# A four-layer diffusion step on one Trainium2 core: where VectorE scales a finished attention output unit in the MLA layers

## The chip, the cores and the metric

The kernel runs on one core of a Trainium2 chip. The metric is the device time of one execution in microseconds (us), the median of several runs. The engines are named as in the profile: PE is TensorE (its matmuls), PEld its weight loads, DVE is VectorE, ACT is ScalarE, POOL is GpSimd, SP is the engine that issues most DMAs. Each engine works through its own queue in order and meets the others through semaphores.

## The reference, cut to what matters

Four layers run one after another on 256 context tokens and 1024 latent tokens, with token mixer `i % 3` in layer i: multi-head latent attention (MLA) in layers 0 and 3, grouped-query attention in layer 1, windowed attention in layer 2. The change touches only the attention of the MLA layers:

```python
def mla_attend(q_nope, q_rope, k_nope, k_rope, v):
    scale = (MLA_NOPE + MLA_ROPE) ** -0.5
    def attend(qn, qr):
        s = (jnp.einsum('bqhd,bkhd->bhqk', qn, k_nope, preferred_element_type=F32)
             + jnp.einsum('bqhr,bkr->bhqk', qr, k_rope, preferred_element_type=F32)) * scale
        p = jax.nn.softmax(s, axis=-1)
        return jnp.einsum('bhqk,bkhd->bqhd', p.astype(v.dtype), v)
    return sweep_queries(attend, (q_nope, q_rope))
...
def finish(o, gate, w_out):
    B, T = o.shape[:2]
    return (o.reshape(B, T, BRANCH) * jax.nn.silu(gate)) @ w_out
```

There are 16 heads. Latent queries read 512 cached, 1024 latent keys; context queries read the 256 context keys.

## The kernel before

`attention` runs one layer's 16 heads in pairs: `pairs_of_heads` writes out the first and the last pair and loops over the six between. In a pair, b is 0 for the first head and 1 for the second. A head has three units of queries: unit 0 and unit 1 are 512 latent queries each, unit 2 is the 256 context queries. The keys are taken in steps of 1024 columns: steps 0 to 5 belong to unit 0, steps 6 to 11 to unit 1, step 12 to unit 2. So a head has NS = 13 steps, a pair P2 = 26.

In step p each engine does, in this order:

- PE: the six score matmuls of step p (L1653), one matmul of the next head's maxima (an "entry", L1461 in `emit_entry`), the six P·V matmuls of step p-2 (L1624 to L1628), and the step's other entries.
- ACT: exp of the scores to `p_f` in float32 (L1711) and again to `p_hi` in float16 (L1715). When a unit's last P·V is done, Ln and Exp make `recip_den`, the reciprocal of the softmax denominators (L1731, L1733), two steps after the unit's last step.
- DVE: the maximum of the step's first entry (L1506 in `take_entry`), then `p_lo` = `p_f` - `p_hi` of step p-1 (L1783), then the maxima of the other entries, and in three of the 13 steps `normed`: `o_f` = the unit's P·V sum times `recip_den` (L1763). In steps 5, 7 and 10 POOL makes `p_lo` in DVE's place (L1856).
- POOL: for each finished unit the gate product (L1838), its float16 part (L1842) and the rest (L1844).

The entries prepare the next head: 26 row maxima of 512 or 256 score columns, three "turns" in which a unit's negated maxima are transposed into the next head's query rows (L1488, copied by ACT at L1538), and, in layer 0 alone, one entry for the next layer's adaLN weights (L1478 or L1426). They are spread over steps 2 to 12 and write two half banks in turn, so an entry's matmul waits until DVE has taken the entry two places earlier. I call the entry with number k "entry k": in layer 0 step 8 holds entries 18, 19, 20, step 9 holds 21, 22 and the turn 23, and step 10 begins with entry 24. In both MLA layers step 2 holds entries 0, 1, 2, and step 3 begins with 3. Entries 0 and 1 are the 256-column maxima of the context queries; entry 1 closes their group, so two small instructions follow it (L1510, L1517).

`normed(i, p)` scales unit 0 in step 8, unit 1 in step 1 of the next head and unit 2 in step 2 of the next head. It waits for `recip_den` and, through `s_og`, for POOL to be done with the `o_f` buffer of two units before. For the second head of a pair it writes partitions 64 to 127 (`rows = slice(HD * b, HD * b + HD)`), for the first head partitions 0 to 63. Its result releases POOL's L1838 and, through `s_o`, the P·V bank and the `recip_den` buffer for the unit after next.

In the MLA layers the order of DVE in a step before was:

```python
take_entry(first) ; p_lo(p - 1) ; take_entry(others) ; normed(i, p)
```

Of the kernel before, what the change touches and what calls it, by code (L numbers as in the profile page):

```python
# [64 lines left out]
def above_zero(value):  # L65

    return not isinstance(value, int) or value > 0
# [19 lines left out]
class Program:  # L87
# [1135 lines left out]
    def attention(self, kind, Q, K, ada_layer, nxt):  # L1223
# [6 lines left out]
        mla, swa = kind == 0, kind == 2  # L1230
# [158 lines left out]
        def pairs_of_heads(eng, body):  # L1389

            if mla:
                peeled(eng, NB, body)
            else:
                for i in range(NB):
                    body(i, i == 0, i == NB - 1)
# [33 lines left out]
        def take_ada(dve, mb, group):  # L1429

            out = A[:, at(group * 3, 3), :]
            dve.tensor_tensor(out, mb[:, 0:6].rearrange("p (r c) -> p r c", r=3),
                              ada_bias[:, at(group * 3, 3)].unsqueeze(2).to_broadcast([P, 3, 2]), ALU.add
                              ).then_inc(s_at.h, 1)
# [56 lines left out]
        def take_entry(dve, hd, b, k):  # L1491
            e = entries[k]
            if e[0] == "ada" and b == 0 and above_zero(hd):
                dve.wait_ge(s_me.h, s_me.base + hd * NE + k + 1)
                take_ada(dve, MB[(b * NE + k) % 2], hd // 2 - 1)
            if e[0] == "ada" and b == 1:
                if above_zero(hd - 1):
                    dve.wait_ge(s_at.h, s_at.base + hd // 2)
                dve.wait_ge(s_me.h, s_me.base + hd * NE + k + 1)
                dve.tensor_copy(rows, MB[(b * NE + k) % 2][:, 0:3 * P]).then_inc(s_ar.h, 1)  # L1500
            if e[0] != "max":
                return
            _, u, t, c, k0, n, masks = e
            par = (3 * b + turn_order[u]) % 2
            dve.wait_ge(s_me.h, s_me.base + hd * NE + k + 1)
            dve.tensor_reduce(mx[:, par, t, c:c + 1], MB[(b * NE + k) % 2][:, 0:n], AX.X, ALU.max).then_inc(s_red.h, 1)  # L1506
            nt = units[u][1] // P
            if t == nt - 1 and c == parts[u] - 1:
                dve.wait_ge(s_red.h, s_red.base + hd * NM + nmax[k + 1])
                dve.tensor_reduce(m4[:, par, 0:nt], mx[:, par, 0:nt, 0:parts[u]], AX.X, ALU.max).then_inc(s_m4.h, 1)  # L1510
                o = turn_order[u]
                dve.wait_ge(s_m4.h, s_m4.base + hd * 3 + o + 1)
                if swa:
                    dve.tensor_scalar(negm[:, par, 0:nt], m4[:, par, 0:nt], sink_raw[:, at(hd)], -1.0 / MAX_UNIT,
                                      ALU.max, ALU.mult).then_inc(s_neg.h, 1)
                else:
                    dve.tensor_scalar(negm[:, par, 0:nt], m4[:, par, 0:nt], -1.0 / MAX_UNIT, None, ALU.mult  # L1517
                                      ).then_inc(s_neg.h, 1)

        def sink_lo(dve, hd, b, o):  # L1520

            q0, nq = units[next(u for u in range(3) if turn_order[u] == o)]
            dve.wait_ge(s_eh.h, s_eh.base + hd * 3 + o + 1)
            dve.tensor_tensor(erow[32:33, b, q0:q0 + nq], es_row[o], erow[0:1, b, q0:q0 + nq], ALU.subtract
                              ).then_inc(s_el.h, 1)
# [19 lines left out]
        with nc.Block() as block:  # L1545
# [192 lines left out]
            @block.vector  # L1738
            def _(dve):
                if swa:  # L1740
                    dve.tensor_scalar(sink_raw[:], sink, 1.0 / scale, None, ALU.mult).then_inc(s_raw.h, 1)
                    dve.wait_ge(s_raw.h, s_raw.base + 1)
                for k in range(NE):
                    take_entry(dve, 0, 0, k)

                def normed(i, p):

                    e = p - 3
                    if e < 0 and i_first[0]:
                        return  # L1750
                    q = e % P2
                    u = steps[q % NS][0]
                    if q % NS != last_of[u]:
                        return
                    un = 3 * (q // NS) + u if e >= 0 else 3 * (q // NS) + u - 6
                    b = q // NS
                    nq = units[u][1]
                    dve.wait_ge(s_rd.h, s_rd.base + i * 6 + un + 1)

                    if above_zero(i * 6 + un - 1):  # L1760
                        dve.wait_ge(s_og.h, s_og.base + i * 6 + un - 1)
                    rows = slice(HD * b, HD * b + HD)
                    dve.tensor_tensor(o32[rows, un % 2, 0:nq], OB[un % 2][0:HD, 0:nq], rden[rows, un % 2, 0:nq],  # L1763
                                      ALU.mult).then_inc(s_o.h, 1)
                i_first = [True]

                def body(i, first, last):
                    i_first[0] = first
                    for p in range(P2 + (3 if last else 0)):
                        b = p // NS  # L1770
                        found = at_step[p % NS] if p < P2 and not (last and p >= NS) else []
                        for k in found[:early]:
                            take_entry(dve, i * 2 + b + 1, 1 - b, k)
                        if p <= P2 and not (first and p == 0) and (p - 1) % P2 % NS not in pooled:

                            q = (p - 1) % P2
                            cols = steps[q % NS][2]
                            g = i * P2 + p - 1
                            dve.wait_ge(s_ph.h, s_ph.base + g + 1)

                            if above_zero(g - back[q] + 1):
                                dve.wait_ge(s_av.h, s_av.base + g - back[q] + 1)
                            dve.tensor_tensor(pl[:, slot[q], 0:cols], p32[:, q % 2, 0:cols], ph[:, slot[q], 0:cols],  # L1783
                                              ALU.subtract).then_inc(s_pl.h, 1)
                        if not mla:
                            normed(i, p)
                        for k in found[early:]:
                            take_entry(dve, i * 2 + b + 1, 1 - b, k)
                        if swa and p < P2:
                            for o in ((0, 1), (2,))[p % NS] if p % NS < 2 else ():  # L1790
                                sink_lo(dve, i * 2 + b, b, o)
                        if mla:
                            normed(i, p)
                    if first:
                        self.next_lo(dve, nx)
                pairs_of_heads(dve, body)
                if ada:
                    dve.wait_ge(s_me.h, s_me.base + HEADS * NE + 1)
                    take_ada(dve, MB[0], KD - 1)
                    dve.wait_ge(s_at.h, s_at.base + KD)  # L1800

                    dve.scalar_tensor_tensor(A[:, KD:2 * KD, :], A[:, KD:2 * KD, :], 1.0,
                                             self.norm_g(ada_layer).unsqueeze(2).to_broadcast([P, KD, 2]),
                                             ALU.add, ALU.mult).then_inc(s_fin.h, 1)
# [321 lines left out]
```

## Time and profile before

| what | value |
| --- | --- |
| runs | 4359.85, 4364.03, 4364.70 us; median 4364.03 us |
| the profiled execution | 4366.46 us, its span 4364.7 us, granted clock 0.959 over the whole span |
| PE busy | 3982.1 us, 91% of the span |
| DVE busy | 2740.2 us, 63% |
| ACT busy | 2399.3 us, 55% |
| POOL busy | 1259.2 us, 29% |
| L1506, maxima on DVE | 1536 instructions, 967.5 us |
| L1783, `p_lo` on DVE | 624 instructions, 757.3 us |
| L1763, `o_f` on DVE | 192 instructions in four layers, 48 in each |

A row of the timeline reads: start, duration, engine, source line, operation, tile written and tile read, shape, count, and in brackets how long the engine sat idle before and what ended that. A pipelined matmul is shown as lasting 0.38 us although the next starts 0.215 us after it, so short pauses of PE do not show as idle time; they are read from the distance between the starts. Layer 0's attention fills about 550 to 1150 us of the span, layer 3's about 3620 to 4240 us.

### The profile page before, as it was taken

Reading aid. Unit: us, or ns where it says so; the run is one execution under the profiler, and the core shown is the slowest. Engines: PE = TensorE matmul, PEld = TensorE weight load, DVE = VectorE, ACT = ScalarE, POOL = GpSimd, SP = SyncE. Lnnn points to the kernel's source line nnn. Section 1 sums busy time; section 2 is a strip of 40 time slices with the busy share of each in tenths; the row PEclk is TensorE's granted clock in tenths of the full one; section 3 lists DMA queues with packets and bytes.
Section 4 is the critical chain, followed back from the end, with each engine's and each line's share of the span. In section 5 each row is a group of like instructions: output and inputs, shape, how many; then the busy total and the mean of one; then the engine's idle time right before and its main releaser. Section 6 shows DMA issues by size and latency. Waiting matters only on the chain. (4 is left out here: it accounts for less than half of the span.)

```text
span 4364.7 us, 58626 instructions
## 1 busy us (share of the span) xinstructions
PE 3982.1 (91%) x20892; PEld 1947.8 (45%) x20892; DVE 2740.2 (63%) x3651; ACT 2399.3 (55%) x3166; POOL 1259.2 (29%) x875
## 2 busy tenths in 40 slices
PE   5997799999999989999999988888999779999998
PEld 1453244444445544444445544444455324444444
DVE  4315477777555738888845528888542447777754
ACT  3325377777634328777833217778332437777761
POOL 1001034434321204444422103333210103444442
PEclk8998799999999989999999989999999879999999
DMA  4124522322202332222111432332111361221211
GB/s 195 49 79 132 161 62 65 76 62 65 73 14 65 116 101 56 62 65 57 45 61 51 123 107 64 83 82 54 57 43 64 110 188 37 55 48 42 54 34 62
DMA packets 375904, 329.39 MB, mean 75 GB/s; under 512 B 247584, under 2 KB 295264, under 8 KB 374544
## 3 DMA queue, kind: packets, MB, share of 16 engines
q1 hardware_dynamic: 375696, 326.60, 26.8%
q8 instruction: 133, 2.18, 0.2%
q14 instruction: 75, 0.61, 0.0%
HBM read 235.30 MB, written 91.23 MB: 75 GB/s over the span
## 5 line engine op out<-in xcount | busy, mean ns | idle before, releaser
L1506 DVE TENSOR_REDUCE max_parts<-bank 128x1 f32<-128x512 f32 (+2 forms) x1536 | 967.5, 656 | 278.7 <-PE bank L1461 254.6
L726 PE MATMUL bank<-H_hilo,w_hilo 128*128 128x512 f16 (+1 forms) x5832 | 1065.7, 346 | 12.4 <-DVE w_hilo L968 8.1
L1711 ACT ACTIVATE p_f<-bank 128x1024 f32<-128x1024 f32 (+2 forms) x768 | 741.3, 965 | 534.0 <-PE bank L1653 487.4
L1653 PE MATMUL bank<-q_slots,k_slots 96*128 96x512 f16 (+7 forms) x3968 | 937.6, 365 | 0.7 <-ACT p_hi L1715 0.6
L1783 DVE TENSOR_TENSOR p_lo<-p_f,p_hi 128x1024 f16<-128x1024 f32 (+2 forms) x624 | 757.3, 1216 | 162.0 <-ACT p_hi L1715 159.0
L726 PEld LDWEIGHTS bank<-H_hilo,w_hilo 128*128 128x128 f16 x5832 | 572.7, 98 | 504.1 <-issue 16.2
L1715 ACT ACTIVATE p_hi<-bank 128x1024 f16<-128x1024 f32 (+2 forms) x768 | 738.3, 961 | 0.0
L1461 PE MATMUL bank<-k_slots,q_slots 96*128 96x512 f16 (+4 forms) x1536 | 542.0, 382 | 111.4 <-DVE max_parts L1506 62.7
L1624 PE MATMUL bank<-p_hi,v_hi_ones 128*128 128x512 f16 (+2 forms) x1568 | 565.3, 362 | 31.1 <-DVE p_lo L1783 18.6
L1626 PE MATMUL bank<-p_hi,v_lo_zeros 128*128 128x512 f16 (+2 forms) x1568 | 565.6, 361 | 0.0
L1628 PE MATMUL bank<-p_lo,v_hi_ones 128*128 128x512 f16 (+2 forms) x1568 | 564.3, 361 | 0.0
L1653 PEld LDWEIGHTS bank<-q_slots,k_slots 96*128 96x128 f16 (+2 forms) x3968 | 375.4, 98 | 397.6 <-issue 24.9
L1838 POOL TENSOR_TENSOR o_gated<-o_f,gate_rows 64x512 f32<-64x512 f32 (+1 forms) x192 | 236.3, 1231 | 846.3 <-DVE o_f L1763 640.2
L1856 POOL TENSOR_TENSOR p_lo<-p_f,p_hi 128x1024 f16<-128x1024 f32 x144 | 316.3, 2197 | 533.6 <-ACT p_hi L1715 510.2
L931 ACT ACTIVATE z_ring<-bank 128x512 f32<-128x512 f32 x328 | 148.7, 531 | 510.3 <-PE bank L726 496.9
L968 DVE SCALAR_TENSOR_TENSOR w_hilo<-w_f,w_hilo 128x1024 f16<-128x1024 f32 (+2 forms) x93 | 114.0, 1227 | 339.0 <-ACT w_hilo L894 337.9
L1461 PEld LDWEIGHTS bank<-k_slots,q_slots 96*128 96x128 f16 (+1 forms) x1536 | 150.4, 98 | 368.4 <-DVE max_parts L1506 168.3
L1049 POOL TENSOR_TENSOR var_rstd<-z_ring,sin 128x1280 f32<-128x1280 f32 x14 | 47.5, 3393 | 662.9 <-ACT z_ring L931 515.0
L1844 POOL TENSOR_TENSOR H_hilo<-o_gated,H_hilo 64x512 f16<-64x512 f32 (+3 forms) x192 | 231.6, 1206 | 23.6 <-POOL H_hilo L1842 13.9
L1624 PEld LDWEIGHTS bank<-p_hi,v_hi_ones 128*128 128x128 f16 x1568 | 152.4, 97 | 191.4 <-DVE p_lo L1783 46.1
L1628 PEld LDWEIGHTS bank<-p_lo,v_hi_ones 128*128 128x128 f16 x1568 | 152.5, 97 | 159.4 <-issue 1.1
L1626 PEld LDWEIGHTS bank<-p_hi,v_lo_zeros 128*128 128x128 f16 x1568 | 153.1, 98 | 141.1 <-issue 0.8
(173 smaller groups left out, 3620.2 us busy)
## 6 DMA issues: line engine op xcount, KB each, us to landing
ada_w<-in_w_ada SPq DMA_DIRECT2D x48, 768.0 KB, 5.7
gate<-z_ring SPq DMA_DIRECT2D x32, 640.0 KB, 2.9
gate_rows<-gate SPq DMA_DIRECT2D x64, 320.0 KB, 4.0
q_slots<-q_mla SPq DMA_DIRECT2D x64, 240.0 KB, 3.2
k_mla<-hilo_out SPq DMA_DIRECT2D x64, 224.0 KB
k_slots<-k_mla SPq DMA_DIRECT2D x64, 224.0 KB, 4.3
v_hi_ones<-v_scratch SPq DMA_DIRECT2D x64, 224.0 KB, 2.9
v_lo_zeros<-v_scratch SPq DMA_DIRECT2D x64, 224.0 KB, 3.5
```

The lines of the kernel that those rows point to most:

```text
L726: ins = pe.matmul(dst, lhs(a, k), rhs(b, k), start=(k == 0 and n == 0), stop=(k == nk - 1 and n == 2))
L1461: ins = pe.matmul(mb[:, 0:n], Q[0:kk, q_slot(hd, b), 0, q0:q0 + P], K[0:kk, k_slot(hd, b), 0, k0:k0 + n], start=True, stop=True)
L1506: dve.tensor_reduce(mx[:, par, t, c:c + 1], MB[(b * NE + k) % 2][:, 0:n], AX.X, ALU.max).then_inc(s_red.h, 1)
L1624: pe.matmul(d, V[:, b, kt], ph[:, slot[q], sel], start=first and n == 0, stop=False, skip_group_check=True)
L1626: pe.matmul(d, VL[:, b, kt], ph[:, slot[q], sel], start=False, stop=False, skip_group_check=True)
L1628: ins = pe.matmul(d, V[:, b, kt], pl[:, slot[q], sel], start=False, stop=fin, skip_group_check=True)
L1653: ins = pe.matmul(dst, lhs, rhs, start=(m == 0), stop=(m == len(ops) - 1), skip_group_check=swa)
L1711: act.activation(p32[:, p % 2, 0:cols], src, ACT.Exp, scale=scale).then_inc(s_p32.h, 1)
L1715: act.activation(ph[:, slot[p], 0:cols], src, ACT.Exp, scale=scale).then_inc(s_ph.h, 1)
L1783: dve.tensor_tensor(pl[:, slot[q], 0:cols], p32[:, q % 2, 0:cols], ph[:, slot[q], 0:cols], ALU.subtract).then_inc(s_pl.h, 1)
L1838: pool.tensor_tensor(og[rows, 0:nq], o32[rows, s, 0:nq], G[rows, q0:q0 + nq], ALU.mult).then_inc(s_og.h, 1)
L1856: pool.tensor_tensor(pl[:, slot[p], 0:cols], p32[:, p % 2, 0:cols], ph[:, slot[p], 0:cols], ALU.subtract).then_inc(s_pp.h, 1)
```

## The change

In `body` of the DVE program, `normed(i, p)` in the MLA layers moves from behind the step's other maxima to the place ahead of them. The other two layers have that order already.

```diff
@@ -1782,15 +1782,12 @@
                             dve.tensor_tensor(pl[:, slot[q], 0:cols], p32[:, q % 2, 0:cols], ph[:, slot[q], 0:cols],
                                               ALU.subtract).then_inc(s_pl.h, 1)
-                        if not mla:
-                            normed(i, p)
+                        normed(i, p)
                         for k in found[early:]:
                             take_entry(dve, i * 2 + b + 1, 1 - b, k)
                         if swa and p < P2:
                             for o in ((0, 1), (2,))[p % NS] if p % NS < 2 else ():
                                 sink_lo(dve, i * 2 + b, b, o)
-                        if mla:
-                            normed(i, p)
```

On DVE, in step 8 of a head (between the `p_lo` of step 6 and that of step 8; the row of five maxima is entries 16 to 20, the single one entry 21):

```order
 L1783 TENSOR_TENSOR p_lo<-p_f_6,p_hi 128x1024 [waits s_pv,s_p_hi]
-L1506 TENSOR_REDUCE max_parts<-bank 128x1 [waits s_max_entry] x5
+L1506 TENSOR_REDUCE max_parts<-bank 128x1 [waits s_max_entry] x3
 L1763 TENSOR_TENSOR o_f_6<-bank,recip_den 64x512 [waits s_rden]
-L1506 TENSOR_REDUCE max_parts<-bank 128x1 [waits s_max_entry]
+L1506 TENSOR_REDUCE max_parts<-bank 128x1 [waits s_max_entry] x3
 L1783 TENSOR_TENSOR p_lo<-p_f_6,p_hi 128x1024 [waits s_pv,s_p_hi]
```

`o_f` of unit 0 now stands behind entry 18 and ahead of entries 19 and 20, which are followed at once by entry 21 and the `p_lo` of step 8.

On DVE, in step 2 of the next head (from the `p_lo` of step 1 to that of step 2; the maxima are entries 1, 2 and 3):

```order
 L1783 TENSOR_TENSOR p_lo<-p_f_6,p_hi 128x1024 [waits s_pv,s_p_hi]
-L1506 TENSOR_REDUCE max_parts<-bank 128x1 [waits s_max_entry]
-L1510 TENSOR_REDUCE max_rows<-max_parts 128x2 [waits s_max_part]
-L1517 TENSOR_SCALAR neg_max<-max_rows 128x2 [waits s_max_row]
-L1506 TENSOR_REDUCE max_parts<-bank 128x1 [waits s_max_entry]
 L1763 TENSOR_TENSOR o_f_6<-bank,recip_den 64x256 [waits s_o_gated,s_rden]
 L1506 TENSOR_REDUCE max_parts<-bank 128x1 [waits s_max_entry]
+L1510 TENSOR_REDUCE max_rows<-max_parts 128x2 [waits s_max_part]
+L1517 TENSOR_SCALAR neg_max<-max_rows 128x2 [waits s_max_row]
+L1506 TENSOR_REDUCE max_parts<-bank 128x1 [waits s_max_entry] x2
```

`o_f` of unit 2 now comes straight behind `p_lo`, ahead of entry 1 with its two small instructions and ahead of entry 2. Unit 1's `o_f` (step 1, in which there are no entries) keeps its place, and so does every instruction of PE, ACT, POOL and SP.

## Rows read from the trace of the kernel before

**Rows 1.** Busy time by engine, one stretch of layer 0: PE, PEld, DVE, ACT, POOL, clock, DMA.

```profile
655.00:764.00 109.00, 108.54 (x536) 48.54 (x534) 85.46 (x128) 78.46 (x95) 46.22 (x34) 1.00 0.28 65
```

**Rows 2.** The line L1763 in layer 0: who waited for it, us and times.

```profile
who waited for it (us, times):
  POOL o_gated L1838: 169.6, 30
```

**Rows 3.** Timeline of PE, layer 0, second head of a pair: steps 8 to 10.

```profile
675.87 0.38 PE L1461 MATMUL bank<-k_slots,q_slots 96*128 96x512 f16 x1
...
677.82 1.46 PE L1653 MATMUL bank<-q_slots,k_slots 96*128 96x512 f16 x6
679.12 0.38 PE L1461 MATMUL bank<-k_slots,q_slots 96*128 96x512 f16 x1
...
681.26 1.48 PE L1653 MATMUL bank<-q_slots,k_slots 96*128 96x512 f16 x6
682.89 0.39 PE L1461 MATMUL bank<-k_slots,q_slots 96*128 96x512 f16 x1 [0.15 <-DVE max_parts L1506]
```

**Rows 4.** Timeline of DVE, the same place.

```profile
676.29 0.69 DVE L1506 TENSOR_REDUCE max_parts<-bank 128x1 f32<-128x512 f32 x1 [0.23 <-PE bank L1461]
677.80 1.29 DVE L1506 TENSOR_REDUCE max_parts<-bank 128x1 f32<-128x512 f32 x2 [0.82 <-PE bank L1461]
679.12 0.68 DVE L1763 TENSOR_TENSOR o_f<-bank,recip_den 64x512 f32<-64x512 f32 x1
679.84 0.69 DVE L1506 TENSOR_REDUCE max_parts<-bank 128x1 f32<-128x512 f32 x1
680.56 1.67 DVE L1783 TENSOR_TENSOR p_lo<-p_f,p_hi 128x1024 f16<-128x1024 f32 x1
682.15 0.68 DVE L1506 TENSOR_REDUCE max_parts<-bank 128x1 f32<-128x512 f32 x1
```

**Rows 5.** Timeline of POOL, the same place.

```profile
679.88 1.26 POOL L1838 TENSOR_TENSOR o_gated<-o_f,gate_rows 64x512 f32<-64x512 f32 x1 [2.76 <-DVE o_f L1763]
681.31 1.39 POOL L1842 CAST H_hilo<-o_gated 64x512 f32 x1 [0.17 <-POOL o_gated L1838]
```

**Rows 6.** Timeline of ACT, the same place: the reciprocal that `o_f` waits for.

```profile
675.48 0.63 ACT L1733 ACTIVATE recip_den<-recip_den 64x512 f32<-64x512 f32 x1
```

**Rows 7.** Timeline of PE, layer 0, next head (first of its pair): step 10.

```profile
721.67 1.48 PE L1653 MATMUL bank<-q_slots,k_slots 96*128 96x512 f16 x6
723.17 0.39 PE L1461 MATMUL bank<-k_slots,q_slots 96*128 96x512 f16 x1
```

**Rows 8.** Timeline of PE, layer 0, step 10 of the second and the fifteenth head.

```profile
599.65 0.38 PE L1653 MATMUL bank<-q_slots,k_slots 97*128 97x512 f16 x1
...
600.68 0.39 PE L1461 MATMUL bank<-k_slots,q_slots 96*128 96x512 f16 x1 [0.65 <-DVE max_parts L1506]
...
1130.07 1.48 PE L1653 MATMUL bank<-q_slots,k_slots 96*128 96x512 f16 x6
1131.72 0.39 PE L1461 MATMUL bank<-k_slots,q_slots 96*128 96x512 f16 x1 [0.18 <-DVE max_parts L1506]
```

**Rows 9.** Timeline, layer 3, steps 1 to 4, as unit 2 of a second head is scaled.

```profile
3768.15 1.23 DVE L1783 TENSOR_TENSOR p_lo<-p_f,p_hi 128x1024 f16<-128x1024 f32 x1 [0.29 <-ACT p_hi L1715]
...
3768.46 0.41 ACT L1733 ACTIVATE recip_den<-recip_den 64x256 f32<-64x256 f32 x1
...
3769.30 0.41 DVE L1506 TENSOR_REDUCE max_parts<-bank 128x1 f32<-128x256 f32 x1
...
3770.16 0.38 PE L1461 MATMUL bank<-k_slots,q_slots 96*128 96x512 f16 x1
...
3770.75 0.42 DVE L1763 TENSOR_TENSOR o_f<-bank,recip_den 64x256 f32<-64x256 f32 x1
...
3771.33 0.72 POOL L1838 TENSOR_TENSOR o_gated<-o_f,gate_rows 64x256 f32<-64x256 f32 x1
...
3771.93 1.22 DVE L1783 TENSOR_TENSOR p_lo<-p_f,p_hi 128x1024 f16<-128x1024 f32 x1
...
3773.81 0.39 PE L1461 MATMUL bank<-k_slots,q_slots 96*128 96x512 f16 x1 [0.17 <-DVE max_parts L1506]
```

## The prediction, made before the changed kernel was run

> **What bounds the kernel now.** I read the busy time by stretch first. In MLA's attention PE is busy 108.5 of 109 us at full granted clock, DVE 85.5, ACT 78.5, POOL 46.2 [rows 1]. So PE sets the time, and the change, which touches DVE alone, can be worth only what PE loses by waiting for DVE. Second, I ask who waits for the moved instruction: in layer 0 only POOL, 30 times, 169.6 us [rows 2], and POOL has that time to spare; PE is not in the list. An earlier `o_f` is therefore worth nothing by itself. What can count is what stands behind it on DVE. PE's pauses are shorter than the 0.16 us by which a shown matmul overlaps the next, so I took the distance from a step's first score matmul to its first entry. Undisturbed it is 679.12 - 677.82 = 1.30 us (six matmuls of 0.217 us) [rows 3]. In layer 0's step 10 it is 682.89 - 681.26 = 1.63, a pause of 0.33 that ended when DVE had taken entry 22 (682.15 + 0.68 = 682.83) [rows 3, 4]. With the head in the other half of the pair it is 723.17 - 721.67 = 1.50, a pause of 0.20 [rows 7].
>
> **Why entry 22 is late.** `o_f` begins at 679.12 and entry 21, whose matmul began at 679.12 as well, is taken only at 679.84. An entry is otherwise taken 676.29 - 675.87 = 0.42 after its matmul starts, so DVE could have had it at 679.54: 0.30 us lost behind `o_f` [rows 3, 4]. Then `p_lo` of step 8 takes 1.67 instead of the 1.23 of a free one [rows 4, 9], because POOL's L1838, released by `o_f`, runs from 679.88 to 681.14 [rows 5]: 681.14 + 1.23 = 682.37 against the end that is shown, 682.23. DVE is held until about 0.14 before the POOL instruction's end and then needs its 1.23.
>
> **Step 8 after the change, layer 0.** Entry 18 is taken by 676.29 + 0.69 = 676.98 [rows 4]. `recip_den` was ready at 675.48 + 0.63 = 676.11 [rows 6], so `o_f` does not wait: 677.01 to 677.69. DVE was idle for 0.82 us there until entry 19 came at 677.80 [rows 4]; the 0.68 of `o_f` fit, with 0.11 to spare. Entries 19 and 20 keep their times, to 679.09. Entry 21: 679.54 to 680.22. POOL starts 2.1 us earlier: L1838 at about 677.77 to 679.03, the cast L1842 (1.39, after 0.17) at 679.20 to 680.59 [rows 5]. `p_lo` of step 8 then starts at 680.14, in the cast's tail. The trace has no `p_lo` that starts under a cast, so two bounds: free, it ends at 681.37; held as under L1838, at 680.59 - 0.14 + 1.23 = 681.68. I take the second, the nearest row being L1838's. Entry 22 is taken by 682.28 at the latest, and PE would need it at 681.26 + 1.30 = 682.56. The pause goes altogether, with over 0.2 us in hand, also in the case of 0.20, where by the same steps entry 22 is done at about 722.6 and PE asks at 722.97.
>
> On this pairwise blocking the Trainium skill ("SBUF — State Buffer", "Who interferes with whom") says that a VectorE instruction with two SBUF inputs and a GpSimd instruction that reads SBUF exclude each other for a whole instruction, whoever starts first. The trace agrees for L1838 with the 1.67 [rows 4, 5]; by that page the cast blocks too, and the sum is the same by it, since both bounds close the pause.
>
> There are 15 such places in layer 0 (the last head prepares no successor). One is larger, 600.68 - 599.65 - 0.22 = 0.81, the last is 1131.72 - 1130.07 - 1.30 = 0.35 [rows 8]; six read about 0.32 as in [rows 3] and seven 0.20 or a little over, as in [rows 7]. Sum: 0.81 + 0.35 + 6 x 0.32 + 7 x 0.21 = 4.5 us. Downstream, scores, exponentials and maxima of steps 10 to 12 all start from PE, so they move forward with it and I expect nothing of it to be given back.
>
> **Step 8 in layer 3.** Without the adaLN entry the numbering is shifted: the turn is entry 21, and step 10's first entry waits for a turn that ACT copies, not for a maximum behind `p_lo`. I found no pause of PE at that entry in any of the 15 places. Gain 0.
>
> **Step 2, both layers.** Here the move delays something. The `p_lo` before it ends at 3768.15 + 1.23 = 3769.38, `recip_den` is ready at 3768.87, and `o_f` (0.42) goes ahead of entry 1 [rows 9]. For a second head, `o_f` starts 0.03 us after the instruction before it has ended and so does the one behind it (679.09 to 679.12, 679.80 to 679.84 [rows 4]), while `p_lo` to entry 1 overlap by 0.08 [rows 9]. So entry 1 is done at 3769.38 + 0.03 + 0.42 + 0.03 + 0.41 = 3770.27 instead of 3769.71; with 0.06 us for the signal (682.83 to 682.89 [rows 3, 4]) PE starts entry 3 at 3770.33 instead of 3770.16: 0.17 us late. It costs little, because in these heads PE stops again a step later, at entry 6, until DVE has taken entry 4 (3773.81 [rows 9]), and that moment is DVE's own: DVE has the same work between the `p_lo` of step 1 and that of step 2 in either order, so that `p_lo` starts at 3771.93 or up to 0.13 earlier, and POOL's L1838 (3771.33 to 3772.05; it starts 0.16 after `o_f` ended instead of the 0.08 of [rows 4, 5], so it waited for POOL's own work and does not move) holds it to 3772.05 - 0.14 + 1.23 = 3773.14, where it ends now (3773.15). In first heads, without the 0.03s and with the overlap kept, entry 1 comes 0.42 - 0.08 = 0.34 later, less than the slack of 3770.16 - 3769.71 - 0.06 = 0.39: nothing. Bounds: 0, and 0.17 x 14 = 2.4 us if the later stop does not swallow it. I take 0.
>
> On the 0.03 us: the Trainium skill ("VectorE: DVE Perf Modes", "Two Vector instructions with no wait between them") has a Vector instruction held until all earlier ones have finished when its output starts in another quadrant of partitions than the last. That is the second head's `o_f`, and the trace agrees with the 0.03 against the overlap of 0.08 [rows 4, 9]. By a rule without it the delay of entry 3 would be about 0.02, and the sum above would not change.
>
> **Sum.** The profiled execution took 4366.5 us; 4366.5 - 4.5 = 4362.0. It lies 2.4 above the median of the runs shown, so for the median 4364.0 - 4.5 = 4359.5 us.
>
> **Rivals.**
> 1. Hidden anyway, no gain. The pause at entry 24 goes but PE meets another within the head, or the `p_lo` of step 8 is held longer than the cast. For it: a pause that is gone brings PE sooner to whatever DVE finishes last next. Against it: what DVE does next (entries 24 and on) starts from PE's own matmuls, which move forward too. Price 0 to +2.4 (the step 2 bound): 4364 to 4366.5.
> 2. Slower: POOL takes the port twice. If, after the cast, POOL's L1844 gets in ahead of the waiting `p_lo` (680.14), and lasts like L1838 (1.26), `p_lo` ends at about 680.59 + 0.17 + 1.26 - 0.14 + 1.23 = 683.1, entry 22 is taken at 683.7, and PE waits 1.2 instead of 0.33: +0.87 x 15 = 13 us in layer 0; I count none in layer 3, where no entry waits behind it. 4364 + 13 = 4377. It decides the matter once `p_lo` ends later than 681.9. Against it: in [rows 4, 5] the `p_lo` that waited under L1838 ran before the cast got its turn, in spite of POOL's pause of only 0.17 between the two.
> 3. Faster: step 2 also improves. If the `p_lo` of step 2, up to 0.13 earlier, gets ahead of POOL's L1838, the stops at entry 6 go too: about 0.33 at each of 15 places in the two layers, 4.9 us. 4359.5 - 4.9 = 4354.6. Against it: `p_lo` would have to start 0.3 earlier.
> That the change does not do what it says can be excluded: the order of DVE's instructions shows it, and only there.
>
> **How the numbers follow.** Chances: forecast 0.66 (4359.5), rival 1 0.22 (4364 to 4366.5), rival 2 0.05 (4377), rival 3 0.07 (4354.6). What a measurement of this kernel can tell from no change is about 0.2%, 8.7 us, hence faster is below 4355.3 and slower above 4372.7. My forecast is a gain of half that size, so "same" is the likely outcome: 0.90; faster 0.05, most of rival 3; slower 0.05, rival 2. Range: from rival 3's 4354.5 to rival 1's upper end, 4367, leaving out rival 2.
>
> **What would show it.** Right: in layer 0's step 10 the distance from the first score matmul to entry 24 falls from 1.63 and 1.50 to 1.30; `o_f` of unit 0 starts right behind entry 18; L1838 starts 2.1 us earlier relative to step 8; the `p_lo` of step 8 lasts 1.23 to 1.6. Entry 3 stands 0.1 to 0.2 later in second heads, and entry 6 where it was. Wrong: a new stop of PE at entry 3 that is not made good by entry 6; a `p_lo` of over 2 us in step 8; or a span of layer 0's attention that is not shorter by 4 to 5 us.

## The result and the profile after

The changed kernel takes 4375.56 us (median of 8 runs, 4370.27 to 4379.46) against 4363.7 us for the kernel before, measured beside it (8 runs, 4359.52 to 4371.18): ratio 1.0026, 95% interval 1.0015 to 1.0037. It is slower by 11.9 us. I had forecast 4359.5, a gain of 4.5 us, with 0.05 on slower.

All of it lies in the attention of the two MLA layers. The line of PE's score matmuls gives the length of each: first and last start of L1653, in the kernel before (layer 0, layer 3) and then in the changed one.

```profile
L1653 PE MATMUL bank<-q_slots,k_slots x1248: 269/379/634, 525.8 to 1171.5; 96*128 96x512 f16 x111, 97*128 97x512 f16 x54, 96*128 96x256 f16 x9, 97*128 97x256 f16 x5
L1653 PE MATMUL bank<-q_slots,k_slots x1248: 270/379/634, 3600.0 to 4234.2; 96*128 96x512 f16 x111, 97*128 97x512 f16 x54, 96*128 96x256 f16 x9, 97*128 97x256 f16 x5
```

```profile
L1653 PE MATMUL bank<-q_slots,k_slots x1248: 269/379/634, 525.1 to 1175.6; 96*128 96x512 f16 x111, 97*128 97x512 f16 x54, 96*128 96x256 f16 x9, 97*128 97x256 f16 x5
L1653 PE MATMUL bank<-q_slots,k_slots x1248: 270/379/634, 3602.6 to 4243.4; 96*128 96x512 f16 x111, 97*128 97x512 f16 x54, 96*128 96x256 f16 x9, 97*128 97x256 f16 x5
```

645.7 + 634.2 = 1279.9 us became 650.5 + 640.8 = 1291.3 us: 11.4 us longer. I use this sum below as "the two stretches". The whole kernel's time differs by several microseconds from run to run, and the stretches leave out what lies outside the attention. But no kernel was profiled twice, and the first head of layer 3 alone takes 40.07 us in one trace and 41.20 in another (the kernel before and e2), so I read nothing into a difference of under 2 us; where less is at stake I go by distances inside the heads.

Now the place that answers to [rows 9], step 2 of layer 3 behind a second head, in the changed kernel: DVE, then POOL, then PE.

```profile
3771.41 1.23 DVE L1783 TENSOR_TENSOR p_lo<-p_f,p_hi 128x1024 f16<-128x1024 f32 x1 [0.29 <-ACT p_hi L1715]
3772.67 0.42 DVE L1763 TENSOR_TENSOR o_f<-bank,recip_den 64x256 f32<-64x256 f32 x1
3773.12 0.42 DVE L1506 TENSOR_REDUCE max_parts<-bank 128x1 f32<-128x256 f32 x1
3773.58 0.15 DVE L1510 TENSOR_REDUCE max_rows<-max_parts 128x2 f32<-128x2 f32 x1
3773.77 0.71 DVE L1517 TENSOR_SCALAR neg_max<-max_rows 128x2 f16<-128x2 f32 x1
3774.39 1.27 DVE L1506 TENSOR_REDUCE max_parts<-bank 128x1 f32<-128x512 f32 x2
3775.58 1.37 DVE L1783 TENSOR_TENSOR p_lo<-p_f,p_hi 128x1024 f16<-128x1024 f32 x1
```

```profile
3773.29 1.15 POOL L1841 TENSOR_TENSOR H_hilo<-o_gated,H_hilo 64x512 f32 x1 [0.18 <-POOL H_hilo L1839]
```

```profile
3772.12 1.46 PE L1653 MATMUL bank<-q_slots,k_slots 96*128 96x512 f16 x6
3773.60 0.39 PE L1461 MATMUL bank<-k_slots,q_slots 96*128 96x512 f16 x1
...
3775.12 0.39 PE L1461 MATMUL bank<-k_slots,q_slots 96*128 96x512 f16 x1
3775.72 0.39 PE L1461 MATMUL bank<-k_slots,q_slots 96*128 96x512 f16 x1 [0.21 <-DVE max_parts L1506]
3775.94 1.46 PE L1653 MATMUL bank<-q_slots,k_slots 96*128 96x512 f16 x6
3777.61 0.39 PE L1461 MATMUL bank<-k_slots,q_slots 96*128 96x512 f16 x1 [0.20 <-DVE max_parts L1506]
```

The row to see is L1517, the negation of two numbers per partition: 0.71 us. It starts at 3773.77, 0.48 us after POOL's third instruction on unit 1 (L1841, L1844 of the kernel before) started, and it ends at 3774.48, 0.04 after POOL's 3774.44. In the kernel before it stood 0.58 us earlier in the step, 0.10 ahead of POOL's, and took 0.17. DVE, then POOL, in the kernel before:

```profile
3769.93 0.17 DVE L1517 TENSOR_SCALAR neg_max<-max_rows 128x2 f16<-128x2 f32 x1
```

```profile
3770.03 1.15 POOL L1844 TENSOR_TENSOR H_hilo<-o_gated,H_hilo 64x512 f32 x1 [0.18 <-POOL H_hilo L1842]
```

Behind a first head the shift is 0.32 us and the negation takes 0.95. After the change DVE is half a microsecond behind: entry 5's matmul comes 3775.72 - 3775.12 - 0.22 = 0.38 late and entry 6's 0.37 (1.67 from the first score matmul instead of 1.30). The stop of entry 6 was there before, 0.33 behind second heads and none behind most first ones; now it is 0.36 behind nearly every head, and layer 3's heads are longer by just what the negation lost: 40.25 us became 40.79 where it takes 0.71 instead of 0.17, and 39.89 became 40.68 where it takes 0.95 (from first score matmul to first score matmul). The group of these negations, 128x2, before and then after (count, busy us, mean ns):

```profile
L1517 DVE TENSOR_SCALAR neg_max<-max_rows 128x2 f16<-128x2 f32 x48 | 16.2, 338 | 1.7
```

```profile
L1517 DVE TENSOR_SCALAR neg_max<-max_rows 128x2 f16<-128x2 f32 x48 | 29.4, 612 | 1.7
```

13.2 us more for 48 instructions, of which 31 lie in the MLA layers. There 23 take 0.54 to 0.78 us longer, and four that had been held for 1.17 us before take 0.33 to 0.58 less. The net is about the size of the loss.

The other place, steps 8 to 10 of a second head of layer 0 (answering to [rows 3 to 5]): DVE, POOL, PE.

```profile
758.06 0.69 DVE L1506 TENSOR_REDUCE max_parts<-bank 128x1 f32<-128x512 f32 x1 [0.23 <-PE bank L1461]
758.78 0.68 DVE L1763 TENSOR_TENSOR o_f<-bank,recip_den 64x512 f32<-64x512 f32 x1
759.57 1.29 DVE L1506 TENSOR_REDUCE max_parts<-bank 128x1 f32<-128x512 f32 x2
761.31 0.69 DVE L1506 TENSOR_REDUCE max_parts<-bank 128x1 f32<-128x512 f32 x1 [0.45 <-PE bank L1461]
762.03 1.97 DVE L1783 TENSOR_TENSOR p_lo<-p_f,p_hi 128x1024 f16<-128x1024 f32 x1
```

```profile
759.54 1.26 POOL L1835 TENSOR_TENSOR o_gated<-o_f,gate_rows 64x512 f32<-64x512 f32 x1 [0.65 <-DVE o_f L1763]
760.97 0.61 POOL L1839 CAST H_hilo<-o_gated 64x512 f32 x1 [0.17 <-POOL o_gated L1835]
761.76 1.16 POOL L1841 TENSOR_TENSOR H_hilo<-o_gated,H_hilo 64x512 f32 x1 [0.18 <-POOL H_hilo L1839]
```

```profile
759.59 1.46 PE L1653 MATMUL bank<-q_slots,k_slots 96*128 96x512 f16 x6
760.89 0.38 PE L1461 MATMUL bank<-k_slots,q_slots 96*128 96x512 f16 x1
...
763.03 1.48 PE L1653 MATMUL bank<-q_slots,k_slots 96*128 96x512 f16 x6
764.65 0.39 PE L1461 MATMUL bank<-k_slots,q_slots 96*128 96x512 f16 x1
```

`o_f` stands where I said, in DVE's idle time behind entry 18, entry 21 is taken 0.42 after its matmul (761.31 after 760.89), and `p_lo` starts 0.30 earlier than before (2.44 after step 9's first score matmul instead of 2.74; I had worked out 0.42). But the cast took 0.61 us, not 1.39. So POOL's third instruction starts at 761.76, ahead of `p_lo`, and holds it: 1.97 us instead of 1.67. Entry 24 comes 1.62 after the first score matmul, as before (1.63). So it is at 12 of the 15 places. At the first two and the last the distance fell, from 1.60, 2.12 and 1.65 to 1.37, 1.31 and 1.43: 1.3 us of the 4.5 that I had forecast.

### The profile page after: what moved, and what is told of

Read it like the earlier page. It is cut to its first block and busy times, and to the rows that moved or that the text cites. A ratio compares the mean times of both kernels' runs of the same rounds, so it can differ in the third digit from the quotient of the medians.

```text
span 4374.2 us, 58626 instructions
## 1 busy us (share of the span) xinstructions
PE 3987.5 (91%) x20892; PEld 1947.8 (45%) x20892; DVE 2752.1 (63%) x3651; ACT 2400.3 (55%) x3166; POOL 1229.2 (28%) x875
## 5 line engine op out<-in xcount | busy, mean ns | idle before, releaser
L1653 PE MATMUL bank<-q_slots,k_slots 96*128 96x512 f16 (+7 forms) x3968 | 938.2, 366 | 0.7 <-ACT p_hi L1715 0.6
L726 PEld LDWEIGHTS bank<-H_hilo,w_hilo 128*128 128x128 f16 x5832 | 571.7, 98 | 501.1 <-issue 10.8
L1653 PEld LDWEIGHTS bank<-q_slots,k_slots 96*128 96x128 f16 (+2 forms) x3968 | 375.7, 98 | 395.1 <-issue 25.0
L1835 POOL TENSOR_TENSOR o_gated<-o_f,gate_rows 64x512 f32<-64x512 f32 (+1 forms) x192 | 225.6, 1175 | 779.8 <-DVE o_f L1763 573.2
L1841 POOL TENSOR_TENSOR H_hilo<-o_gated,H_hilo 64x512 f16<-64x512 f32 (+3 forms) x192 | 256.1, 1334 | 23.6 <-POOL H_hilo L1839 13.9
```

Of the source, the lines that this page charges most:

```text
L726: ins = pe.matmul(dst, lhs(a, k), rhs(b, k), start=(k == 0 and n == 0), stop=(k == nk - 1 and n == 2))
L1653: ins = pe.matmul(dst, lhs, rhs, start=(m == 0), stop=(m == len(ops) - 1), skip_group_check=swa)
L1841: pool.tensor_tensor(H(1), og[rows, 0:nq], H(0), ALU.subtract).then_inc(s_ol.h, 1)
```

## The experiments

The theory from the two traces, A: the loss is the negation L1517, held by POOL's instruction since it starts behind it; unit 0's move gives and costs next to nothing. Rivals: B, the longer hold of step 8's `p_lo` costs the time; C, both parts share it; D, DVE's new order costs by itself (maxima taken later), whatever POOL does. All rows below are medians and ratios to the kernel before measured beside them (a ratio is made from all the runs and need not be that of the two medians); the last column is the two stretches of one profiled execution.

| kernel | us | before, beside it | ratio (95%) | two stretches, us |
| --- | --- | --- | --- | --- |
| before | | | | 1279.9 |
| changed | 4375.56 | 4363.7 | 1.0026 (1.0015 to 1.0037) | 1291.3 |
| e1 unit 2 early | 4380.21 | 4366.5 | 1.0031 (1.0018 to 1.0043) | 1292.7 |
| e2 unit 0 early | 4362.94 | 4366.5 | 0.9993 (0.9984 to 1.0002) | 1279.2 |
| e3 unit 2 in the middle | 4371.54 | 4366.5 | 1.0008 (0.9999 to 1.0017) | 1283.6 |
| e4 both a step later | 4370.64 | 4366.5 | 1.0010 (1.0001 to 1.0019) | 1283.2 |
| e5 changed, unit 1's POOL work cut | 4369.0 | 4366.24 | 1.0002 (0.9992 to 1.0011) | 1280.5 |
| e6 before, the same cut | 4364.35 | 4366.24 | 0.9993 (0.9983 to 1.0002) | 1275.7 |
| e7 unit 0 early, unit 0's POOL work cut | 4361.74 | 4366.24 | 0.9989 (0.9979 to 0.9998) | 1273.9 |
| e8 before, the same cut | 4364.91 | 4366.24 | 0.9998 (0.9988 to 1.0009) | 1279.0 |
| e9 changed, other negation | 4360.85 | 4366.15 | 0.9988 (0.9979 to 0.9997) | 1275.7 |
| e10 before, other negation | 4364.99 | 4366.15 | 0.9997 (0.9989 to 1.0006) | 1276.8 |
| e11 unit 2 a step later | 4361.79 | 4366.15 | 0.9990 (0.9981 to 0.9998) | 1275.8 |
| e12 combined | 4359.61 | 4366.15 | 0.9984 (0.9975 to 0.9993) | 1272.2 |
| e13 before, maximum and negation in one | 4353.29 | 4366.92 | 0.9968 (0.9956 to 0.9980) | 1271.1 |
| e14 combined, and in one | 4347.92 | 4366.92 | 0.9957 (0.9943 to 0.9970) | 1263.1 |

### The two parts apart: e1 and e2

`normed` gets the units it may scale as an argument. In e1 unit 2 alone goes ahead, in e2 unit 0 alone:

```diff
                         if not mla:
                             normed(i, p)
+                        else:
+                            normed(i, p, (2,))      # e2: (0,)
                         for k in found[early:]:
                             take_entry(dve, i * 2 + b + 1, 1 - b, k)
...
                         if mla:
-                            normed(i, p)
+                            normed(i, p, (0, 1))    # e2: (1, 2)
```

> One part of the change alone: in the MLA layers only unit 2's o_f (step 2) goes ahead of the step's other maxima, unit 0's stays behind them. Theory A (the whole loss is in step 2: the 128x2 negation L1517 now starts after POOL's third instruction of unit 1 has started and lasts 0.7 to 0.95 us instead of 0.17): the time of the changed kernel, about 12 us over the kernel before, with L1517 at 0.7 to 0.95 in the trace. Theory B (the loss comes from the longer shadow on the p_lo of step 8, unit 0): no change, 4364. Theory C (both halves share it): 3 to 9 us over.

> The other part alone: only unit 0's o_f (step 8) goes ahead, unit 2's stays behind. Theory A: within 1.5 us of the kernel before; the pauses at entry 24 in layer 0 stay at about 0.31 and 0.19 us because the p_lo of step 8 (1.7 to 2.0 us) is now held by POOL's third instruction instead of its first. Theory B: all of the 12 us. The forecast's own sum would have been -4.5 us.

e1 has the whole loss (1.0031, stretches +12.8 us) and e2 none: stretches -0.7 us, ratio at most 1.0002 by its interval. Its median is 3.6 us under the kernel before, where I had expected 1.5 at most; the interval holds both. B and C fall.

### Between the two: e3

```diff
                         for k in found[early:]:
                             take_entry(dve, i * 2 + b + 1, 1 - b, k)
+                            if mla and k == 1:
+                                normed(i, p, (2,))
```

> Unit 2's o_f goes between the two: behind entry 1 and its two small instructions (L1510, L1517), ahead of entry 2; unit 0's stays behind. Theory A: L1517 keeps its old start, ahead of POOL's third instruction, lasts 0.17 us, and the time is that of the kernel before within 1.5 us. Rival D (any o_f ahead of a maximum in step 2 costs, since entry 2 and with it entry 3 come later): 4 us or more over.

The negation is back at 0.17 us, and most of the loss is gone; but 3.7 us of stretch and 5.0 of the median remain, where theory A had 1.5 at most and rival D 4 or more. The trace of layer 3 behind a first head shows where: DVE, then POOL, then PE.

```profile
3815.15 0.17 DVE L1517 TENSOR_SCALAR neg_max<-max_rows 128x2 f16<-128x2 f32 x1
3815.32 0.42 DVE L1763 TENSOR_TENSOR o_f<-bank,recip_den 64x256 f32<-64x256 f32 x1
3815.66 1.27 DVE L1506 TENSOR_REDUCE max_parts<-bank 128x1 f32<-128x512 f32 x2
3816.86 1.49 DVE L1783 TENSOR_TENSOR p_lo<-p_f,p_hi 128x1024 f16<-128x1024 f32 x1
```

```profile
3816.54 0.73 POOL L1840 TENSOR_TENSOR o_gated<-o_f,gate_rows 64x256 f32<-64x256 f32 x1
```

```profile
3817.43 1.46 PE L1653 MATMUL bank<-q_slots,k_slots 96*128 96x512 f16 x6
3819.01 0.39 PE L1461 MATMUL bank<-k_slots,q_slots 96*128 96x512 f16 x1
```

`p_lo` of step 2 starts 0.32 us after POOL's first instruction on unit 2 (L1838 of the kernel before) and is held, 1.49 us. In the kernel before, at the same place, it started 0.25 after it and it was POOL that waited:

```profile
3811.72 1.21 DVE L1783 TENSOR_TENSOR p_lo<-p_f,p_hi 128x1024 f16<-128x1024 f32 x1
```

```profile
3811.47 2.04 POOL L1838 TENSOR_TENSOR o_gated<-o_f,gate_rows 64x256 f32<-64x256 f32 x1
```

With the other loser of this meeting comes a stop of PE of 3819.01 - 3817.43 - 1.30 = 0.28 us at entry 6, behind the first heads of layer 3, whose lengths grew by 0.30. The start alone does not settle who loses: with 0.25 us between the two starts the kernel before has eight meetings in the MLA layers that `p_lo` won and one that it lost (742.07, 1.55 us), while at 0.28 us and over it lost in every run. What remains of the loss is for the most part this hold, the same as A's on another instruction. It does come with DVE's new order, though, so e3 leaves a small D open.

### POOL's instruction cut short: e5 to e8

If POOL's third instruction is what holds the negation (unit 1) and step 8's `p_lo` (unit 0), it must help to make it short. It is cut to 16 of 512 columns for one unit, in the changed order and, as a control, in the order before:

```diff
-                    pool.tensor_tensor(H(1), og[rows, 0:nq], H(0), ALU.subtract).then_inc(s_ol.h, 1)
+                    if mla and u in (1,):           # e7, e8: (0,)
+                        L = lambda c: self.H[rows, c, at(i - 1 if un < 0 else i), q0:q0 + 16].rearrange("p a n -> p (a n)")
+                        pool.tensor_tensor(L(1), og[rows, 0:16], L(0), ALU.subtract).then_inc(s_ol.h, 1)
+                    else:
+                        pool.tensor_tensor(H(1), og[rows, 0:nq], H(0), ALU.subtract).then_inc(s_ol.h, 1)
```

> The changed kernel, with POOL's third instruction of unit 1 (L1844 of before) cut in the MLA layers to 16 of its 512 columns: the low half of unit 1's gated output is left out but for 16 columns. Theory A: with nothing on POOL to hold it, the negation L1517 is back at 0.17 us although it starts as late as in the changed kernel, entry 6 waits at most 0.1 us, and the time falls by 10 us or more against the changed kernel, to that of the kernel before or a few us under it. Rival D (the loss comes from DVE's order itself, not from POOL): 4370 or more.

> The control: the kernel before with the same cut (unit 1's low half left out but for 16 columns). Theory A: little changes, since L1517 is not held there: 4364 down to 4360, the latter because POOL's first instruction of unit 2 starts earlier and frees the p_lo of step 2 sooner.

> Only unit 0's o_f ahead, with POOL's third instruction of unit 0 cut to 16 of 512 columns in the MLA layers (the low half of unit 0's gated output is left out but for them). Theory A: the p_lo of step 8 lasts 1.23 us, the pauses of 0.31 and 0.20 us at entry 24 go, and the forecast's 4.5 us appear: 4357 to 4361. Rival (those pauses have another cause than the held p_lo): 4364, pauses unchanged.

> The control: the kernel before with the same cut of unit 0. Theory A: the p_lo of step 8 is held by POOL's first instruction, which is uncut, so it lasts 1.67 or 1.91 us as before and the pauses at entry 24 stay: 4364 within 2 us.

Unit 1: the cut takes 10.8 us of stretch from the changed kernel and 4.2 from the one before, so the move costs 11.4 with the instruction and 4.8 without it. The expectation of 10 us or more is met in the stretches; the ratio falls from 1.0026 to 1.0002, the distance of the medians from 11.9 to 2.8 us. The negation did not go back to 0.17 everywhere, nor entry 6's wait to 0.1: behind second heads the negation took 0.64 us, since it now ran into POOL's next instruction, the first on unit 2, which had moved up (0.72 us, begun 0.10 us before it at 3766.01 of e5), and entry 6 still waited 0.35. Behind first heads both were free, and those heads took 39.84 us in layer 3, as short as in the kernel before.

Unit 0: this is the forecast's own step, with the cause of its failure taken away. Layer 0, the same place as above, in e7: DVE, POOL, PE.

```profile
761.60 1.22 DVE L1783 TENSOR_TENSOR p_lo<-p_f,p_hi 128x1024 f16<-128x1024 f32 x1
```

```profile
760.54 0.61 POOL L1844 CAST H_hilo<-o_gated 64x512 f32 x1 [0.17 <-POOL o_gated L1840]
761.33 0.22 POOL L1848 TENSOR_TENSOR H_hilo<-o_gated,H_hilo 64x16 f32 x1 [0.18 <-POOL H_hilo L1844]
```

```profile
762.60 1.48 PE L1653 MATMUL bank<-q_slots,k_slots 96*128 96x512 f16 x6
763.91 0.38 PE L1461 MATMUL bank<-k_slots,q_slots 96*128 96x512 f16 x1
```

1.31 us between the last two: the pause at entry 24 is gone, at all 15 places, and e7 is 5.1 us of stretch under e8 (1273.9 against 1279.0), all of it in layer 0: the forecast's 4.5. The medians are 3.2 us apart, and e7's 4361.74 lies just above the 4357 to 4361 expected. Without the cut, e2, it was 0.7 us of stretch under the kernel before.

### The same order, another instruction: e9 and e10

The sharpest test leaves order and POOL alone and only exchanges the held instruction. A tensor_reduce over an axis of one element, with negation, does what the tensor_scalar did; the factor 1/16 moves into the row of K that multiplies it.

```diff
-                pool.memset(K[row:row + 1, :, 1, :], MAX_UNIT).then_inc(s_row.h, 1)
+                pool.memset(K[row:row + 1, :, 1, :], 1.0 if kind == 0 else MAX_UNIT).then_inc(s_row.h, 1)
...
+                elif mla:
+                    dve.tensor_reduce(negm[:, par, 0:nt], m4[:, par, 0:nt].unsqueeze(2), AX.X, ALU.max, negate=True
+                                      ).then_inc(s_neg.h, 1)
                 else:
                     dve.tensor_scalar(negm[:, par, 0:nt], m4[:, par, 0:nt], -1.0 / MAX_UNIT, None, ALU.mult
```

> The changed kernel, with nothing moved and POOL untouched; only the negation of the maxima in the MLA layers (L1517, 128x2 and 128x4, float32 in SBUF to float16 in SBUF) is done by a tensor_reduce over an axis of one element with negation instead of a tensor_scalar (the factor 1/16 goes into the constant row of K, which is 1 instead of 16). Same place, same size, same result. Theory A (POOL's third instruction of unit 1 holds the tensor_scalar, and only that is the loss): the 128x2 negation lasts under 0.25 us everywhere, MLA heads return to within 0.1 us of the kernel before (40.8 and 40.2 us), the time falls by about 10 us against the changed kernel. Rival D (the later start of the negation and of the maxima itself costs, whatever the instruction): still 8 us or more over the kernel before.

> The control: the kernel before with the same exchange of the negation. Theory A: in the loop nothing changes, since the negation was not held there (0.17 us); only the first and the last 128x2 negation of a layer (1.17 us before) fall: 0 to -3 us.

Layer 3, step 2 in e9: DVE, then POOL.

```profile
3758.81 0.16 DVE L1510 TENSOR_REDUCE max_rows<-max_parts 128x2 f32<-128x2 f32 x1
3759.00 0.15 DVE L1517 TENSOR_REDUCE neg_max<-max_rows 128x2 f16<-128x2 f32 x1
```

```profile
3758.52 1.16 POOL L1844 TENSOR_TENSOR H_hilo<-o_gated,H_hilo 64x512 f32 x1 [0.18 <-POOL H_hilo L1842]
```

The negation starts 0.48 us after POOL's instruction, exactly as in the changed kernel, and takes 0.15 us instead of 0.71. The stretches are 15.6 us under the changed kernel's, 1275.7 against 1276.8 in the control; the median was 11.9 us over the kernel before beside it and is now 5.3 under. With this one instruction exchanged, the moved order costs nothing in sum: A stands, and D falls as the cause of the loss. The gain is more than the 10 us I had written down; the ends of a layer gain too (the control has 3.1 us less stretch than the kernel before), for the rest I have no cause. A small cost of the order is still there under that sum: in e9 the `p_lo` of step 2 loses to POOL behind the first heads of layer 3 (1.56 us, begun 0.24 after POOL), as in e3, and six of the seven heads behind these take 40.11 or 40.12 us, against 39.87 to 40.15 in e10: 1.0 us in all. So D is right to that extent.

### The other direction, and a version that beats both: e4, e11, e12

e4 scales units 0 and 2 one step later, at the end of steps 9 and 3, so that POOL's work on them begins behind the `p_lo` that it held:

```diff
-                    for p in range(P2 + (3 if last else 0)):
+                    for p in range(P2 + ((4 if mla else 3) if last else 0)):
...
                         if mla:
-                            normed(i, p)
+                            normed(i, p, (1,))
+                            normed(i, p, (0, 2), 4)     # e = p - 4 instead of p - 3
```

> The opposite direction: o_f of unit 0 and of unit 2 one step later, at the end of steps 9 and 3, behind the p_lo of step 8 and of step 2, so that POOL's work on the unit starts after these p_lo and can't hold them. Theory A (what costs PE its pauses at entry 24 in layer 0 and at entry 6 is a p_lo held by POOL): the pauses of 0.31 and 0.20 and those of 0.33 go, 4 to 9 us faster than the kernel before. Rival: POOL's work now falls on the p_lo of steps 9 and 3 and the pauses move there: no change. Rival: the later unit delays POOL's own p_lo of step 10 (2.2 us) beyond PE's need: slower by 5 us or more.

The second rival came true in kind, with 4.1 us in the medians and 3.3 in the stretches where it had 5 or more. The pauses at entries 24 and 6 went at nearly every place, but layer 3 grew by 5.4 us (layer 0: -2.1). Its step 12 in e4, DVE, POOL, PE:

```profile
3797.82 0.64 DVE L1517 TENSOR_SCALAR neg_max<-max_rows 128x4 f16<-128x4 f32 x1
```

```profile
3796.31 2.12 POOL L1857 TENSOR_TENSOR p_lo<-p_f,p_hi 128x1024 f16<-128x1024 f32 x1 [0.22 <-POOL H_hilo L1845]
```

```profile
3798.51 0.38 PE L1488 MATMUL bank<-const_f,neg_max 128*1 128x128 f16 x4 [1.00 <-DVE neg_max L1517]
```

Unit 0's later work pushed POOL's own `p_lo` of step 10 back onto another negation, for which PE waits 1.00 us (0.53 in the kernel before, where that `p_lo` ended 1.7 us ahead of the negation): the same collision in a third place. So e11 delays unit 2 alone, and e12 also lets unit 0 go early on DVE while POOL takes it up behind its `p_lo` of step 10 (`unit_at = [10 if mla else 8]`).

> Only unit 2's o_f one step later, at the end of step 3; unit 0's and all of POOL's order as in the kernel before. Theory A: the p_lo of step 2 is free, the stops at entries 5 and 6 go, heads shorten by 0.2 us in both layers, 5 to 7 us under the kernel before; the loss that the two-unit version had in step 12 (0.3 and 0.5 us a head) came from unit 0 alone and is absent. Rival: that loss comes from unit 2's delay: heads of layer 3 at 40.5 us, no gain or a loss.

> A version meant to beat both: unit 0's o_f early as in the change, but POOL takes up unit 0 only behind its own p_lo of step 10 (so nothing of POOL's runs beside the p_lo of step 8), and unit 2's o_f one step later. Theory A: pauses at entry 24 in layer 0 go (4.5 us) and those at entries 5 and 6 too (5 to 7 us), step 12 stays as before: 8 to 12 us under the kernel before. Rival (POOL's work on unit 0, now beside steps 11 and 12, holds their p_lo, or the next P.V waits for it): within 3 us of it.

e11: -4.1 us of stretch and -4.4 in the median (expected 5 to 7), e12: -7.7 and -6.5 (expected 8 to 12), ratio 0.9984. Both signs as expected, both sizes a little under. In step 2 of layer 0 e12's heads are 0.16 us longer on average than before; why, I did not find out, and that step differs by up to 0.07 between kernels that leave it alone (before and e8).

### One link less in the chain: e13 and e14

```diff
+                if mla:
+                    dve.tensor_reduce(negm[:, par, 0:nt], mx[:, par, 0:nt, 0:parts[u]], AX.X, ALU.max, negate=True
+                                      ).then_inc(s_neg.h, 1)
+                    return
                 dve.tensor_reduce(m4[:, par, 0:nt], mx[:, par, 0:nt, 0:parts[u]], AX.X, ALU.max).then_inc(s_m4.h, 1)
```

> The kernel before, with the row maximum (L1510) and the negation (L1517) of the MLA layers made one instruction: a tensor_reduce with negation straight to float16 (constant row of K 1 instead of 16). Nothing is moved. If the chain behind the last maximum sets the stop of 0.69 us in step 12 of layer 3, that stop falls by the 0.2 us of one link: heads of layer 3 at 39.9 to 40.0 us, 3 to 5 us under the kernel before in all. If it does not: 4364 within 2 us.

> e12 and e13 together. If the gains add: 4 us under e12, 10 to 12 us under the kernel before (heads about 40.4 and 39.7 us). If they replace each other (the same stops): as e12, 6 to 7 us under it.

e13: 8.8 us of stretch less, 7.0 of them in layer 3, where the wait for the turn in step 12 shrank by the link's 0.2 us and a wait of 0.14 at step 8's first entry went as well; I had expected 3 to 5 us. Of the 8.8, e10 has 3.1 from the other operation alone, so the missing link is worth about 5.7. The median shows 13.6 us. Its interval, 8.7 to 19.2 us, reaches down to the 8.8, so whether anything lies outside the stretches is not shown. e14: 16.8 us of stretch less, ratio 0.9957, 19.0 us under the kernel before in the median, the fastest version of the study. The gains add (7.7 + 8.8 = 16.5), and this is more than the 10 to 12 expected, since e13 had gained more.

## Why the prediction was wrong, point by point

**The bound and who waits.** Right: PE sets the time, nothing but POOL waits for `o_f` in these layers, and what counts is what stands behind it on DVE. Both moves did to `o_f`, entry 18 to 21 and `recip_den` what was worked out; only `p_lo` of step 8 came 0.12 us later, since it started 0.03 behind entry 21 and not 0.08 under it.

**Step 8, layer 0: a pause that would go, -4.5 us.** Wrong, for it was -1.3; and the term of the sum that failed is the length of the cast, "L1842 (1.39, after 0.17)". That row had been stretched by the very `p_lo` it overlapped; alone the cast takes 0.61 us. The trace of before had such rows, in the attention of layer 1: the cast from 1644.97 to 1645.57 is one. The `p_lo` that starts at 1645.30, under this cast, and lasts 1.36 us is one of the rows of which the prediction says that the trace has none; it agrees with the second bound (1645.57 - 0.14 + 1.23 = 1646.66). The groups of casts of that shape, before and after (count, busy us, mean ns):

```profile
L1842 POOL CAST H_hilo<-o_gated 64x512 f32 x48 | 67.0, 1396 | 8.3 <-POOL o_gated L1838 8.3
```

```profile
L1839 POOL CAST H_hilo<-o_gated 64x512 f32 x48 | 47.5, 990 | 8.3 <-POOL o_gated L1835 8.3
```

With 0.61, by the prediction's own steps, the cast ends at 679.81, L1844 starts at 679.99, before `p_lo` (680.14), and the hold lasts to the end of that one. Rival 2 had the right instruction (L1844 holds `p_lo`) with the wrong way there, so a price of 13 us; the true hold ended `p_lo` where it had ended before, 4.41 us after step 9's first score matmul, and nothing was gained at 12 of the 15 places. e7 shows that the rest of the step was sound: 5.1 us came once L1844 was out of the way.

**Step 8, layer 3: 0.** Right; e2 shows 634.8 us against 634.2.

**Step 2: the step that decided, "I take 0", with 2.4 us as the bound.** By e1 it was +12.8 us of stretch; with the -1.3 of step 8 that makes 11.5, against 11.4 measured. Wrong in "DVE has the same work between the `p_lo` of step 1 and that of step 2 in either order". The list of instructions is the same, their durations are not. I priced the delay of entry 1 and of the PE matmul behind it (0.17 expected, 3773.60 - 3772.12 - 1.30 = 0.18 measured behind second heads in layer 3; in layer 0 entry 3 was late once), and passed over L1517, which I never costed where it would stand. It was shifted by 0.58 us behind second heads and 0.32 behind first ones, into POOL's L1844, and lost 0.54 to 0.78 us in nearly every head. With it went the statement that entry 6's stop would stay where it was. All the slower side of my distribution rested on a `tensor_tensor` being held; I had not thought of a `tensor_scalar` of two elements as something that can be held.

The trace of before held the warning. At the very place of [rows 9], rows 3769.93 and 3770.03 above, only 0.10 us lay between the negation and L1844 behind it, and the move was to push the negation back by more than that. At the first pair of heads of layer 0, where the order of arrival is different, DVE and POOL read:

```profile
575.44 1.17 DVE L1517 TENSOR_SCALAR neg_max<-max_rows 128x2 f16<-128x2 f32 x1
```

```profile
575.42 1.15 POOL L1844 TENSOR_TENSOR H_hilo<-o_gated,H_hilo 64x512 f16<-64x512 f32 x1
```

A 0.17 us instruction that takes 1.17 when POOL's starts 0.02 us ahead of it. The line's group gave it away too, with a mean of 338 ns where the rows I looked at showed 170.

**The page that bears on it.** I had quoted the Trainium skill for the pair `tensor_tensor` and POOL. The same section of the Trainium skill ("SBUF — State Buffer", "Who interferes with whom") lists `tensor_scalar` among the VectorE operations that can take both ports when their operands allow it, and `tensor_reduce` as one that on trn2 never contends. The runs agree with both: 0.71 against 0.15 us at the same place (e9). The rule I cited for one instruction should have been run over every instruction that the move shifts.

**The chances.** 0.05 on slower was too little, and the range's upper end, 4367, ended where my own list of mechanisms ended. That rival 2's 4377 lies near the measured 4375.6 is an accident: it was to come from step 8.

## What to carry to other kernels

When an instruction moves, recompute for each instruction between its old and its new place when it will start and what runs on GpSimd at that moment, small ones above all: on a pair of engines that exclude each other, a shift of a few tenths of a microsecond turns 0.17 us into 0.7, or decides which of two waits. Take durations for such a sum from a row that ran alone, since a row beside its rival contains the wait; a group's mean above the typical row is a sign of it. And look whether a link can be done by an operation that takes no part in the exclusion (here a tensor_reduce with negation in place of a tensor_scalar): in the changed order that took back the whole loss. Merged with the maximum before it, in the order of before, it gained more (8.8 us of stretch) than any order tried (7.7).

## What the runs showed of the hardware that I had not expected

- A `tensor_scalar` of 128x2 elements, float32 to float16 in SBUF, waits for a whole GpSimd `tensor_tensor` that started before it: 1.17 us when it started 0.02 us behind, 0.95 when 0.23 behind, 0.71 when 0.48 behind, 0.17 alone. The same work as a `tensor_reduce` took 0.15 to 0.16 us in all 96 cases of the MLA layers in e9, in 28 of them begun while that GpSimd instruction ran.
- Which of two `tensor_tensor` waits is not settled by the recorded starts: VectorE's started 0.25 us after GpSimd's and went first in eight of nine cases of the kernel before (GpSimd's lasted 2.04 instead of 0.72 us); the ninth was held, and e9 has eight held at 0.24. At 0.32 us, in e3, it was held each time (1.49 instead of 1.21).
- A GpSimd cast of 64x512, 0.61 us alone, is recorded as 1.36 us (3771.75 of the changed kernel) when a VectorE `tensor_tensor` of 1.23 us started 0.34 us before it: it ends 0.47 after the VectorE one. So a recorded GpSimd duration can hold time in which it waited.
